# Weighted sum of gathered expert rows: diagonal matmuls replaced by ScalarE scaling and accumulating fp32 transposes

## What is computed

```python
def block(xb):                                   # 128 tokens
    qh = (xb @ w_pq).reshape(PEER_BLOCK, PEER_HEADS, 2, PEER_HALF)
    sc = jnp.einsum('thcq,hckq->thck', qh, sub_keys).astype(F32)
    ...                                          # top 16 of 16 x 16 sums: eidx, softmax gates g
    u = jnp.take(peer_u, eidx, axis=0)
    a = jax.nn.gelu(jnp.einsum('thkd,td->thk', u, xb).astype(F32), approximate=False)
    vsel = jnp.take(peer_v, eidx, axis=0)
    return jnp.einsum('thk,thkd->td', (g * a).astype(xb.dtype), vsel)
...
x = x + gt2 * peer(h2.reshape(Bx * L, D), w_pq, sub_keys, peer_u, peer_v).reshape(Bx, L, D)
```

## Time and profile before

| what | us |
|---|---|
| median of three runs | 3890.75 |
| lowest and highest run | 3866.1, 3899.0 |
| span of the profiled execution | 3871.8 |
| PE busy in it (records of matmul) | 3160.2 |
| DVE busy | 2662.3 |
| ACT busy | 571.9 |
| POOL busy | 1136.8 |
| q0, the gathers: share of 16 DMA engines over the span | 68.8% |

### The profile page before, as it was taken

The page is one execution under the profiler, slowest core; times in us unless marked ns, Lnnn a source line. Parts: engine busy times, 40 slices in busy tenths (PEclk is TensorE's granted clock), DMA queues, the critical chain, the costliest instruction groups (busy, mean ns, idle before and its releaser), DMA issues.

```text
span 3871.8 us, 34246 instructions
## 1 busy us (share of the span) xinstructions
PE 3160.2 (82%) x9119; PEld 1451.9 (37%) x9119; DVE 2662.3 (69%) x7007; ACT 571.9 (15%) x1352; POOL 1136.8 (29%) x1089
## 2 busy tenths in 40 slices
PE   8999999999667787877777777787877778777877
PEld 2455545555123333333333333333333333333332
DVE  0333234444138888888888888888888888888887
ACT  0221122222101111111111111111111111111110
POOL 0000000000003443434344443443434434443443
PEclk9888899999879999999999999999999999999999
DMA  8566665543748999999999999999999999999998
GB/s 304 206 222 223 222 222 199 195 158 121 268 165 353 422 403 404 422 403 422 400 401 421 394 422 401 422 399 400 422 392 422 394 401 415 396 422 391 422 395 351
DMA packets 264243, 1337.34 MB, mean 345 GB/s; under 512 B 23680, under 2 KB 24032, under 8 KB 130832
## 3 DMA queue, kind: packets, MB, share of 16 engines
q0 software_dynamic: 152832, 1096.88, 68.8%
q1 hardware_dynamic: 111376, 240.00, 17.0%
HBM read 1318.03 MB, written 18.77 MB: 345 GB/s over the span
## 4 chain that ended last, share of the span: by engine, by line
DVE 30%; DMA 15%; issue 12%; PE 10%; ACT 3%; POOL 0%; DVEq 0%; ACTq 0%; POOLq 0%; SPq 0%
DMA pr_ring<-uv,pr_expert 15%; DVE pr_ring L1439 12%; PE pair L1321 8%; DVE pr_diag L1453 4%; DVE pr_act_h L1448 2%; DVE pr_pos L1361 2%; ACT pr_act_h L1223 2%; DVE pr_work L1360 2%; DVE pr_pos L1365 2%; DVE pr_top L1359 1%; DVE pr_top L1364 1%; DVE pr_dot L1439 1%; DVE pr_half_pos L1379 1%; DVE pr_cand L1374 1%; PE bank L1254 0%
## 5 line engine op out<-in xcount | busy, mean ns | idle before, releaser
L1321 PE MATMUL pair<-pr_ring,pr_diag 128*128 128x512 f32 x4096 | 1917.9, 613 | 565.3 <-DVE pr_diag L1453 557.9
L1146 POOL DMA_INDIRECT pr_ring<-uv,pr_expert x1024 | 1091.5, 1066 | 1610.7 <-PE pair L1321 1387.4
L1321 PEld LDWEIGHTS pair<-pr_ring,pr_diag 128*128 128x128 f32 x4096 | 752.2, 193 | 1633.8 <-DVE pr_diag L1453 855.3
L1439 DVE CUSTOM_DVE_ANT_0 pr_ring<-pr_ring,pr_h2cur 128x1024 f32<-128x1024 f32 x1024 | 1222.7, 1223 | 144.2 <-DMA pr_ring<-uv,pr_expert 88.8
L1223 ACT ACTIVATE pr_act_h<-pr_dot 128x2 f32<-128x2 f32 x512 | 104.1, 203 | 2209.0 <-DVE pr_dot L1439 2208.9
L578 PE MATMUL pair<-sb_w,sb_hT 128*128 128x512 f32 x896 | 388.6, 592 | 1.4 <-ACT sb_gt2row L289 1.4
L1453 DVE TENSOR_SCALAR pr_diag<-sb_ident,pr_act_h 128x128 f32<-128x128 f32 x1024 | 256.4, 296 | 18.0
L578 PEld LDWEIGHTS pair<-sb_w,sb_hT 128*128 128x128 f32 x896 | 168.9, 190 | 208.4 <-issue 208.4
L1448 DVE SCALAR_TENSOR_TENSOR pr_act_h<-pr_act_h,pr_gsum,pr_gate_h 128x2 f32<-128x2 f32 x512 | 114.3, 223 | 143.3 <-ACT pr_act_h L1223 143.3
L252 POOL DMA_DIRECT2D x_mid<-sb_qk x8 | 4.9, 610 | 496.2 <-DVE sb_sp L505 496.2
L1254 PEld LDWEIGHTS bank<-pr_wpq,pr_h2T 128*128 128x128 f32 x1088 | 133.5, 194 | 40.9 <-issue 31.0
(11 more groups left out here) (300 smaller groups left out, 2236.2 us busy)
## 6 DMA issues: line engine op xcount, KB each, us to landing
sb_w<-w_in SPq DMA_DIRECT2D x56, 2048.0 KB, 8.3
sb_w<-w_out SPq DMA_DIRECT2D x16, 2048.0 KB, 7.7
sb_w<-w_ada SPq DMA_DIRECT2D x12, 2048.0 KB, 7.8
pr_ring<-uv,pr_expert POOLq DMA_INDIRECT x1024
de_w<-w_in SPq DMA_DIRECT2D x7, 2048.0 KB, 12.8
sb_xt<-x_all SPq DMA_DIRECT2D x9, 512.0 KB, 11.1
pr_h2next<-h SPq DMA_DIRECT2D x9, 512.0 KB
sb_mix<-x_all SPq DMA_DIRECT2D x8, 512.0 KB, 3.3
```

What stands on the lines that cost most here:

```text
L1146: pool.indirect_dma_start(ring[r][:], None, a["uv"], bass.IndirectOffsetOnAxis(ap=index, axis=0)).then_inc(s_g[r], 16)
L1321: last = pe.matmul(psS[0][:, c], diag[:, s, :], ring[s % RING][:, D + c.start:D + c.stop], start=False, stop=False, skip_group_check=True)
L1439: last = dve.tensor_tensor_reduce(ring[r][:, 0:D], ring[r][:, 0:D], h2cur[:], 1.0, 0.0, ALU.mult, ALU.add, dot[:, s:s + 1])
```

## The change

The value rows are now multiplied by their coefficients in place on ACT, one 128x1024 scaling for a slot (`weigh`). PE then transposes each slot's `v` half in 8 blocks of 128x128 against the identity and lets the transposes accumulate in PSUM, so that `psS[0]` holds the transposed sum. At the tile's end DVE multiplies that by the transposed `gt2` (`tabs[:, 5]`) into `yT`, PE turns it back in 8 transposes into `psS[1]`, and DVE adds `x_mid`. The diagonals, `ysum` and `gt2row` are gone. `weigh` of group q stands on ACT behind the gelu of group q+1; that of the last group stands at the end of the head.

```diff
@@ peer, ACT
+            def weigh(n, q):
+                act.wait_ge(s_coef, n * GROUPS + q + 1)
+                for s in range(q * GRP, q * GRP + GRP):
+                    last = act.activation(ring[s % RING][:, D:2 * D], ring[s % RING][:, D:2 * D], ACT.Identity,
+                                          scale=act_h[:, s:s + 1])
+                last.then_inc(s_dg, 1)
...
                                 act.activation(act_h[:, c], dot[:, c], ACT.Gelu).then_inc(s_gelu, 1)
+                                if q >= 1:
+                                    weigh(n, q - 1)
                                 if q == 2:
                                     query_out(n + AHEAD)
...
-                act.wait_ge(s_y, t + 1)
-                act.wait_ge(s_st, t * 16 + 1)
-                act.activation(ysum[:], psS[0][:], ACT.Copy).then_inc(s_yc, 1)
+                            weigh(n, GROUPS - 1)
@@ peer, PE
                                 for s in range(q * GRP, q * GRP + GRP):
-                                    for half in range(2):
-                                        c = slice(half * 512, half * 512 + 512)
-                                        last = pe.matmul(psS[0][:, c], diag[:, s, :],
-                                                         ring[s % RING][:, D + c.start:D + c.stop],
-                                                         start=False, stop=False, skip_group_check=True)
+                                    for k in range(KT):
+                                        last = pe.matmul(psS[0][:, k * P:(k + 1) * P],
+                                                         ring[s % RING][:, D + k * P:D + (k + 1) * P], ident[:],
+                                                         start=False, stop=False, is_transpose=True,
+                                                         skip_group_check=True)
                                 last.then_inc(s_free, 1)
...
                 last.then_inc(s_y, 1)
+                pe.wait_ge(s_yc, t + 2)
+                for k in range(KT):
+                    last = pe.transpose(psS[1][:, k * P:(k + 1) * P], yT[:, k, :], ident[:])
+                last.then_inc(s_yT, 1)
@@ peer, DVE
-                            dve.wait_ge(s_coef, n * GROUPS + q + 1)
-                            for s in range(q * GRP, q * GRP + GRP):
-                                last = dve.tensor_scalar(diag[:, s, :], ident[:], act_h[:, s:s + 1], None, ALU.mult)
-                            last.then_inc(s_dg, 1)
                             choose_next(q, n + 2, u)
                 restart()

-                dve.wait_ge(s_yc, t + 2)
+                dve.wait_ge(s_y, t + 1)
+                dve.tensor_tensor(yT[:], psS[0][:].rearrange("p (k i) -> p k i", k=KT),
+                                  tabs[:, 5, :, B:B + 1].to_broadcast([P, KT, P]), ALU.mult).then_inc(s_yc, 1)
                 dve.wait_ge(s_xm, t * 16 + 16)
-                step(dve.tensor_tensor(ysum[:], ysum[:], gt2row[:], ALU.mult))
-                dve.tensor_tensor(ysum[:], ysum[:], xmid[:], ALU.add).then_inc(s_out, 1)
+                dve.wait_ge(s_yT, t + 1)
+                dve.tensor_tensor(xmid[:], psS[1][:], xmid[:], ALU.add).then_inc(s_out, 1)
@@ peer, SP
-                sp.wait_ge(s_out, t + 1)
+                sp.wait_ge(s_st, t * 16 + 1)
                 sp.dma_start(xmid[:], a["x_mid"][ds(t * P, P), :]).then_inc(s_xm, 16)
                 sp.wait_ge(s_out, t + 2)
-                sp.dma_start(a["y_prompt"][ds(t * P, P), :], ysum[:]).then_inc(s_st, 16)
+                sp.dma_start(a["y_prompt"][ds(t * P, P), :], xmid[:]).then_inc(s_st, 16)
@@ front: the fourth broadcast row, gt2row, is not made any more (on DVE, PE and ACT)
```

More of the change, by code:

```diff
@@ L69, in build, with front @@
         mod = keep("mod", [P, 48, NC9])
-        gt2row = keep("gt2row", [P, D])
         tabs = keep("tabs", [P, 6, KT, NC9])
-        front(nc, a, sem, ps, psS, psO, ident, mod, gt2row, tabs)
+        front(nc, a, sem, ps, psS, psO, ident, mod, tabs)
         decode(nc, a, sem, ps, psS, psO, ident, tabs)
-        peer(nc, a, sem, ps, psS, psO, ident, gt2row)
-def front(nc, a, sem, ps, psS, psO, ident, mod, gt2row, tabs):
+        peer(nc, a, sem, ps, psS, psO, ident, tabs)
+def front(nc, a, sem, ps, psS, psO, ident, mod, tabs):
     with ExitStack() as ctx:
@@ L286, in _ @@
             x_turned(0)
-            for n, row in enumerate((gt1row, a2row, b2row, gt2row)):
+            for n, row in enumerate((gt1row, a2row, b2row)):
                 act.wait_ge(s_bc, n + 1)
@@ L368, in _ @@
             dve.wait_ge(s_tabs, 2)
-            for n, sec_no in enumerate((2, 3, 4, 5)):
+            for n, sec_no in enumerate((2, 3, 4)):
                 dve.tensor_tensor(diagonals[n][:].rearrange("p (k i) -> p k i", k=KT),
@@ L374, in _ @@
             dve.wait_ge(s_init, 4)
-            dve.wait_ge(s_row, 4)
+            dve.wait_ge(s_row, 3)
             for first in range(0, T, SEG):
@@ L543, in _ @@
             pe.wait_ge(s_init, 4)
-            for n in range(4):
+            for n in range(3):
                 pe.wait_ge(s_diag, n + 1)
@@ L553, in _ @@
                 last.then_inc(s_bc, 1)
-            pe.wait_ge(s_row, 4)
+            pe.wait_ge(s_row, 3)
             for first in range(0, T, SEG):
@@ L998, in _, with peer @@
             dve.tensor_tensor(h2s[:], h2s[:], rows[:, 2, :], ALU.add).then_inc(s_h2, 1)
-def peer(nc, a, sem, ps, psS, psO, ident, gt2row):
+def peer(nc, a, sem, ps, psS, psO, ident, tabs):
     AHEAD = 4
@@ L1018, in peer @@
         xmid = sb("xmid", [P, D])
-        ysum = sb("ysum", [P, D])
-        diag = sb("diag", [P, TOPK, P])
+        yT = sb("yT", [P, KT, P])
         zeros = sb("zeros", [P, P])
@@ L1080, in peer @@
         s_coef = sem("expert_weights")
-        s_dg = sem("diagonals")
+        s_dg = sem("values_weighted")
+        s_yT = sem("peer_sum_turned_back")
         s_free = sem("ring_free")
```

## The result

The changed kernel takes 4309.99 us, the median of four runs (4304.89 to 4318.88), against 3892.07 for the kernel before: a ratio of 1.109, 95% interval 1.1049 to 1.1131. It is 418 us slower where 486 were forecast, and both the direction and the mechanism of the forecast hold.

A forecast was written before the change was run, and what follows sets the result against it. DMA bounds the kernel before; after the change the four-pair ring is too short. (5.83-4.97) x 512 = 440 us, plus 48 for stops, less 2 at the front: +486, giving 4377, stated as 4375 us; range 4130 to 4520.

The forecast's parts named there:

- the late scaling in a ring of four pairs: Expert stage: scaling after the next pair's gelu holds slots one period longer; period 5.83 against 4.97 us, 440 us more.
- The expected signs: Changed profile: DMA 340 to 370 GB/s, more dot waits, transposes 1.9 or 3.7 us, ACT +1100 us, refill after 11 to 14.
- The scaling: ACT, two in-place 128x1024 scalings per pair: 1.15 us each, 2.3 a pair, 0.26 more or less at the ends.
- Issue and transfer: From POOL's issue to the landing of a pair's two slots: 10.2 us, between 7.9 and 11.2.
- The half clock for six tenths of the stage: PE in the expert stage: half clock for six tenths of it, an estimate, giving a period of 5.93 us.
- The period: Landing to landing of pairs in the expert stage: 5.93 us, less 0.1 for a head's last pair, 5.83.
- The stops: Short DMA stops, two in each of eight tiles: growing by 3 us each, 48 in all (0 to 6 each).
- the half clock throughout (A): PE at the half clock all through the expert stage: period 6.07 us, 4500 us; chance 0.17 together with D.
- The full clock (B): PE at the full clock throughout the expert stage: period 5.48 us, 4198 us; chance 0.17.
- The ring that still covers (C): Round trip under 14.9 us, DMA stays at 422 GB/s, not slower: 3845 us, or 3800 without stops; chance 0.06.
- Transposes in two passes (D): PE issues each transpose as two passes, 16 take 3.7 us at full clock: 4500 us; chance 0.17 together with A.

The follow-up runs named there:

- the filler: Two matmuls of zeros 128x512 into an unused PSUM bank after each pair's transposes, added to the changed kernel; 4274.79 us, ratio 1.0997.
- the third pass: Changed kernel with an extra ACT pass of 128x1024 into a spare buffer ahead of each pair's two scalings; 4441.01 us, ratio 1.1429.
- the scaling at once: Changed kernel with each pair's scaling right behind its own gelu on ACT, eight slots kept; 3862.69 us, ratio 0.9931.

## Why the prediction was right, and where its sizes were off

The forecast was the late scaling in a ring of four pairs, and that is what the runs show: move the scaling and the loss is gone, lengthen the ring and it is gone, put the late release alone into the kernel before and it is there.

- *The expected signs.* The slices (340 to 370 forecast, 336 to 366 found), the dots' wait for the DMA, 16 transposes in 1.97 or 3.67 us, a refill 13.1 us after its landing (11 to 14), and 1106 us more of ACT are all in the profile of the changed kernel.
- *The scaling*, taken at 1.15 us each between 1.02 and 1.28, measured 1133 ns, and 2.17 us for two, since the second starts before the first has ended. The row of the in-place Exp was the right one to stand nearest to.
- *Issue and transfer*, 10.2 us, was somewhat too long: 8.4 and the 1.24 between two issues are 9.6.
- *The half clock for six tenths of the stage.* A mean clock of 0.74 between the levels 0.5 and 1 is 0.52. PE holds 1481.3/512 = 2.89 us a pair where the sum had 2.97.
- *The period.* Between the turns 357 GB/s are 2.097/357 = 5.87 us a pair; 5.83 was forecast. Over 512 pairs that is 20 us too little, so this term came out nearly as it was summed. Part of that is luck. Transfer, scaling and transposes were counted 0.6, 0.13 and 0.08 us too long; a third of the three in 512 periods is 138 us, and something that the sum doesn't have stands in their place. One thing that it left out is the start of a head, of which these rows show one:

```profile
2429.74 4.25 ACT L1190 ACTIVATE pr_ring<-pr_ring,pr_act_h 128x1024 f32<-128x1024 f32 x4
...
2433.35 1.22 DVE L1450 CUSTOM_DVE_ANT_0 pr_ring<-pr_ring,pr_h2cur 128x1024 f32<-128x1024 f32 x1 [0.79 <-DMA pr_ring<-uv,pr_expert]
...
2434.01 1.28 ACT L1225 ACT_TABLE_LOAD   x1
...
2435.63 1.28 ACT L1230 ACT_TABLE_LOAD   x1
2436.92 0.20 ACT L1230 ACTIVATE pr_act_h<-pr_dot 128x2 f32<-128x2 f32 x1
```

ACT has four scalings and two table loads to do before the head's first gelu, which starts 3.57 us after its second dot (2.81 in the mean over the heads without a turn) and not 1.27 as in all other pairs, and DVE waits with it. How much of the 138 us that is stays open.
- *The stops.* This is the term that was mis-sized. The sum left the 90 us of stops of the kernel before in place and added 48. In the changed kernel 512 pairs at 5.87 are 3005 us and the blocks 30, so of the stage's 3095 us some 60 are left for stops where 138 stood. They shrank and did not grow. The stop at a tile's end has not gone (25 GB/s above), but a pair that is late there is late in a ring that is behind anyway. That last reason is argued; no run isolates it.

Together +20 and -78 leave the sum 58 us too high; 4377 - 58 = 4319 stands beside the measured 4310.

Of the rivals, the half clock throughout (A) falls: transposes in 1.97 us and a mean of 0.74 show the full clock granted for almost half of the stage. The Trainium skill, TensorE: Matmul & The Clock Gate, Part 4, would have transposes leave the clock at half. By that the time would have been 4500. This trace does not agree. Here are three rows of PE's timeline in the changed kernel and two stretches of the same time:

```profile
2374.93 0.60 PE L1272 MATMUL bank<-pr_subk,pr_qhT 128*128 x2
2376.50 1.97 PE L1327 MATMUL pair<-sb_ident,pr_ring 128*128 128x128 f32 x16 [0.98 <-ACT pr_ring L1190]
2383.45 6.15 PE L1327 MATMUL pair<-sb_ident,pr_ring 128*128 128x128 f32 x32 [4.97 <-ACT pr_ring L1190]
...
2382.00:2388.00 6.00, 4.55 (x22) 4.56 (x23) 2.66 (x7) 5.95 (x8) 0.07 (x1) 0.50 0.97 395
2388.60:2389.60 1.00, 0.99 (x10) 0.75 (x7) 0.49 (x2) 0.01 (x1) 0.69 (x2) 1.00 1.02 393
```

After a pause of 4.97 us the clock was at 0.50, 32 transposes ran, and before they had ended 1.00 was granted, with no other matmul since 2375.53. The full clock (B) was neared by the filler, which gave 77 us between the turns and 35 in all. The ring that still covers (C) is not what the changed kernel does, but it is what happened as soon as the scaling was put behind its own gelu: 3863, between the 3845 that it was priced at with half of the stops gone and the kernel before. Transposes in two passes (D) falls with 1.97 us.

The prediction priced a microsecond of hold by the ring's length alone, 171 us. The runs say 126 to 138. By that price the terms of the clock and of the scaling mattered less than I weighed them.

## What to carry to other kernels

Where a ring feeds the DMA, count how long a slot is held, from its landing to the issue of its refill, and add the transfer: that sum over the number of buffers that are refilled together (four pairs here) is about the period, if it is longer than the transfer itself needs, whatever the engines' busy shares are. It is a first count: here it gave 22.7/4 = 5.68 us for one pair where 5.87 was the mean. An engine that is nearly idle can then cost 11% merely by doing its part one turn of the loop later. Before a step is moved to an idler engine, either place it so that the hold doesn't grow or make the ring longer first. And read the rate between the ends of blocks and the rate around them apart, over all blocks: a mean over both says of neither how it changed.

## What I had not expected of the hardware

- The time from a gather's issue to its landing is no constant: the same 1 MB gather took 8.0 us with the third pass, 8.4 in the changed kernel, 10.1 with the scaling at once and 24.4 with sixteen slots, at 336 (over its stage), 350, 408 and 422 GB/s. It grows as the gathers are issued earlier, and so takes back part of what a shorter hold gives.
- A starved DMA shows no even lower rate but full speed with holes: 406 to 439 GB/s, and 39 in between. The page's slices, 108 us wide, show only the mean.
- Transposes alone brought the granted clock from 0.50 to 1.00 (at 2388 us of the changed kernel).
- ACT's scaling of 128x1024 fp32 in place took the same 1133 ns beside a DMA at 350 GB/s as 1140 ns at 408.
